# Decay matrices of two token mixers: mask and row spread accumulated on TensorE in three single-pass products, exponentials read from the accumulator bank

## Reference

```python
# mLSTM, per chunk, head and direction
dlog = jnp.where(_causal(t), bt[..., :, None] - bt[..., None, :] + it[..., None, :], -jnp.inf)
m_t = jnp.maximum(m_inter, jnp.max(dlog, -1))
s = jnp.exp(dlog - m_t[..., None]) * jnp.einsum('bnthk,bnshk->bnhts', q, k)
# SSD
seg = jnp.where(_causal(t), at[..., :, None] - at[..., None, :], -jnp.inf)
y = jnp.einsum('bnhts,bnshp->bnthp', jnp.exp(seg) * cb, xdt)
```

## Time and profile before

| | |
|---|---|
| median of 3 runs | 2839.63 us (2838.87 to 2845.24) |
| the profiled execution | 2846.07 us, its span 2844.3 us |
| mean granted TensorE clock | 0.921 of full speed |
| mLSTM rounds, layer 0 | 748.2 to 825.6 us of the span |
| SSD rounds, layer 0 | 962.2 to 1082 us |
| mLSTM rounds, layer 1 | 2140.6 to 2203.1 us |
| SSD rounds, layer 1 | 2317.9 to 2402 us |

### The profile page before, as it was taken

One profiled execution on the slowest core, in us unless ns is written; L12 is line 12 of the kernel. 1 busy time (PEld: TensorE's weight loads), 2 busy tenths in 40 slices (PEclk: granted clock), 3 DMA queues, 4 the chain that ended last, 5 costly groups with the idle time before them and its releaser, 6 DMA issues. The chain is left out here.

```text
span 2844.3 us, 37711 instructions
## 1 busy us (share of the span) xinstructions
PE 2462.7 (87%) x13246; PEld 2249.5 (79%) x13246; DVE 1356.0 (48%) x1923; ACT 1060.0 (37%) x1631; POOL 1394.5 (49%) x604
## 2 busy tenths in 40 slices
PE   5699989898778887799998999899987787789997
PEld 2499988777556676799998999787775767779997
DVE  4554252563655426664326541526455533765424
ACT  4333245334433353253225322452443323243322
POOL 3365545465434674355554555455642322536553
PEclk8799999999878898899999999999997888989999
DMA  8443323233332452233332333233432212214332
GB/s 274 141 140 126 119 96 126 90 127 119 116 109 81 152 162 83 89 109 127 114 124 101 128 110 121 93 108 119 134 111 75 83 65 67 91 66 140 126 116 69
DMA packets 93459, 323.16 MB, mean 114 GB/s; under 512 B 11040, under 2 KB 14368, under 8 KB 92960
## 3 DMA queue, kind: packets, MB, share of 16 engines
q1 hardware_dynamic: 87552, 312.03, 33.3%
q10 hardware_dynamic: 5792, 9.56, 1.0%
HBM read 317.35 MB, written 4.20 MB: 113 GB/s over the span
## 5 line engine op out<-in xcount | busy, mean ns | idle before, releaser
L518 POOL TENSOR_TENSOR wlo<-raw,whi 128x1024 fp32r<-128x1024 f32 (+2 forms) x600 | 1394.3, 2332 | 1417.3 <-ACT whi L972 1355.2
L972 ACT CAST whi<-raw 128x1024 fp32r<-128x1024 f32 (+1 forms) x600 | 615.4, 1036 | 1003.7 <-PE ps L552 666.4
L550 PE MATMUL ps<-h_hi,whi 128*128 128x384 f32 x2224 | 765.6, 344 | 34.6 <-DVE h_lo L2023 13.3
L551 PE MATMUL ps<-h_lo,whi 128*128 128x384 f32 x2224 | 754.4, 339 | 0.0
L552 PE MATMUL ps<-h_hi,wlo 128*128 128x384 f32 x2224 | 754.0, 339 | 0.0
L550 PEld LDWEIGHTS ps<-h_hi,whi 128*128 128x128 f32 x2224 | 427.2, 192 | 45.3 <-DVE h_lo L2023 13.9
L551 PEld LDWEIGHTS ps<-h_lo,whi 128*128 128x128 f32 x2224 | 427.0, 192 | 2.8 <-issue 2.2
L552 PEld LDWEIGHTS ps<-h_hi,wlo 128*128 128x128 f32 x2224 | 426.0, 192 | 0.0
L550 PE MATMUL ps<-act_hi,whi 128*128 128x384 f32 x704 | 242.1, 344 | 11.5 <-DVEq L458 6.0
L552 PE MATMUL ps<-act_hi,wlo 128*128 128x384 f32 x704 | 240.5, 342 | 0.0
L551 PE MATMUL ps<-act_lo,whi 128*128 128x384 f32 x704 | 240.3, 341 | 0.0
(11 more groups left out here) (311 smaller groups left out, 3113.3 us busy)
## 6 DMA issues: line engine op xcount, KB each, us to landing
raw<-in_w_in SPq DMA_DIRECT2D x248, 512.0 KB, 3.4
raw<-in_w_gu SPq DMA_DIRECT2D x176, 512.0 KB, 3.4
raw<-in_w_down SPq DMA_DIRECT2D x64, 512.0 KB, 3.4
raw<-in_w_mod SPq DMA_DIRECT2D x40, 512.0 KB, 4.4
raw<-in_w_down SPq DMA_DIRECT2D x32, 384.0 KB, 2.9
raw<-in_w_branch SPq DMA_DIRECT2D x24, 512.0 KB, 3.4
raw<-in_w_out SPq DMA_DIRECT2D x16, 512.0 KB, 3.5
x<-in_x ACTq DMA_DIRECT2D x1, 1536.0 KB, 6.5
```

Source lines behind the costliest of these rows:

```text
L518: nc.gpsimd.tensor_tensor(wlo[s][:, 0:w], raw[s][:, 0:w], whi[s][:, 0:w].bitcast(F32), ALU.subtract).then_inc(w_split, 1)
L550: mm(out, hi_, xh[:, xc, :], start=start and n == 0, stop=False)
L551: mm(out, hi_, xl[:, xc, :], start=False, stop=False)
L972: act.copy(whi[m][:, 0:w], raw[m][:, 0:w]).then_inc(w_hi, 1)
```

## The change

Three things move. `spread` becomes three products of single-pass type (F32R) accumulated in the bank: the identity by the mask (broadcast over the three blocks), the broadcast identity column by the high part `x_5h` of the rows, and by their low part `x_5l`. `exps` and its buffers `pt` go; `pair` reads the bank and waits for PE, and PE waits for `pair` before it overwrites a bank. The identity and the mask become F32R tiles, filled by two DVE copies at the start, and DVE makes `x_5h` and `x_5l` in "rows". Uses of `ident` elsewhere read the same tile as fp32.

```diff
-        ident = sb("ident", [P, P])
+        ident_r = sb("ident_r", [P, P], F32R)
+        ident = ident_r[:, :].bitcast(F32)
...
-        neg = sb("neg", [P, 2, P])
+        neg = sb("neg", [P, 2, P], F32R)
...
-        (pt0, pt1, pr0, pr1, st0, st1), e3 = region(
-            rows0, *[(n, [P, T]) for n in ("pt0", "pt1", "pr0", "pr1", "st0", "st1")])
+        (x_5h, x_5l, pr0, pr1, st0, st1), e3 = region(
+            rows0, ("x_5h", [P, T], F32R), ("x_5l", [P, T], F32R), *[(n, [P, T]) for n in ("pr0", "pr1", "st0", "st1")])
...
-            def spread(r, rr):
-
+            def spread(r, d, rr):
+
+                out = ps[r % 2][:, 0:T]
                 if r >= 2:
-                    pe.wait_ge(pr_x, r - 1)
-                mm(ps[r % 2][:, 0:T], ident[:, rr:rr + 1].to_broadcast([P, P]), x_5[:, :], start=True,
-                   stop=True).then_inc(pr_bc, 1)
+                    pe.wait_ge(pr_e, r - 1)
+                mm(out.rearrange("p (a b) -> p a b", b=P), ident_r[:, :], neg[:, d:d + 1, :].to_broadcast([P, NT, P]),
+                   start=True, stop=False)
+                row = ident_r[:, rr:rr + 1].to_broadcast([P, P])
+                mm(out, row, x_5h[:, :], start=False, stop=False)
+                mm(out, row, x_5l[:, :], start=False, stop=True).then_inc(pr_bc, 1)
...
             def pair(r, rr):
-                act.wait_ge(pr_x, r + 1)
+                act.wait_ge(pr_bc, r + 1)
...
-                    last = af(pr[r % 2][:, c], pt[r % 2][:, c], ACT.Exp, bias=t_1[:, t, rr:rr + 1])
+                    last = af(pr[r % 2][:, c], ps[r % 2][:, c], ACT.Exp, bias=t_1[:, t, rr:rr + 1])
...
             cp(hmask[:, :, :, :], hmask_in[:, :, :, :])
+            cp(ident_r[:, :], ident_in[:, :])
+            cp(neg[:, :, :], neg_in[:, :, :])
...
                 dve.wait_ge(row_d, 3)
+                step.done()
+                step(cp(x_5h[:, :], x_5[:, :]))
+                step.done()
+                step(tt(x_5l[:, :], x_5[:, :], x_5h[:, :].bitcast(F32), ALU.subtract))
                 dve.wait_ge(row_a, 5)
...
-            def exps(r, d):
-                dve.wait_ge(pr_bc, r + 1)
-                if r >= 2:
-                    dve.wait_ge(pr_e, r - 1)
-                tt(pt[r % 2][:, :].rearrange("p (a b) -> p a b", b=P),
-                   neg[:, d:d + 1, :].to_broadcast([P, NT, P]),
-                   ps[r % 2][:, 0:T].rearrange("p (a b) -> p a b", b=P), ALU.add).then_inc(pr_x, 1)
...
-                exps(0, 0)
                 for r in range(8):
-                    if r < 7:
-                        exps(r + 1, (r + 1) % 2)
                     scores(r, ps[2], r // 2 + 1)
...
-                exps(8, 0)
                 for r in range(16):
                     scores(8 + r, ps[2], 5 + r // 8, 64 + 32 * (r % 2) + r // 2)
-                    if r < 15:
-                        exps(9 + r, (r + 1) % 2)
                     skipped(r)
```

More of the change, by code:

```diff
@@ L201, in build @@
         tb, sbf, vb, sq, ht = (tb0, tb1), (sb0, sb1), (vb0, vb1), (sq0, sq1, sq2, sq3), (ht0, ht1, tb0)
-        (pos, hmask_in), _ = region(arena, ("pos", [P, KC, NL_TOK]), ("hmask_in", [P, 2, len(LEVELS) + 1, P]))
+        (pos, hmask_in, ident_in, neg_in), _ = region(
+            arena, ("pos", [P, KC, NL_TOK]), ("hmask_in", [P, 2, len(LEVELS) + 1, P]), ("ident_in", [P, P]),
+            ("neg_in", [P, 2, P]))
         (mq, mk, va), hg0 = region(arena, ("mq", [P, NH, T]), ("mk", [P, NH, T]), ("va", [P, NT, NH, C1]))
@@ L248, in build @@
         (kw0, kw1), _ = region(e6 - 2 * T * 4, ("kw0", [P, 2, P]), ("kw1", [P, 2, P]))
-        pt, pr, st, kw, co = (pt0, pt1), (pr0, pr1), (st0, st1), (kw0, kw1), (co0, co1)
+        pr, st, kw, co = (pr0, pr1), (st0, st1), (kw0, kw1), (co0, co1)
         (xt, bt), _ = region(e6 - 2 * T * 4 - 2048 - NT * MIX * 4 - 9312, ("xt", [P, NT, MIX]), ("bt", [P, NT, P]))
@@ L339, in build @@
         pr_bc = signal("pe", "pr_bc")
-        pr_x = signal("dve", "pr_x")
         pr_e = signal("act", "pr_e")
@@ L670, in normed @@
                     for g in range(NH):
-                        last = nc.tensor.transpose(ps[2 + t % 2][:, g * P:(g + 1) * P], nyn[:, g, :], ident[:, :])
+                        last = nc.tensor.transpose(ps[2 + t % 2][:, g * P:(g + 1) * P], nyn[:, g, :], ident)
                     last.then_inc(nm_tr, 1)
@@ L704, in keys_turned @@
                         last = nc.tensor.transpose(ps[2 + s % 2][:, g * P:(g + 1) * P],
-                                                   kk[:, d, g, t * P:(t + 1) * P], ident[:, :])
+                                                   kk[:, d, g, t * P:(t + 1) * P], ident)
                     last.then_inc(hg_t, 1)
@@ L749, in rows @@
                         last = nc.tensor.transpose(ps[i % 2][:, t * P:(t + 1) * P], xi[:, t * P:(t + 1) * P],
-                                                   ident[:, :])
+                                                   ident)
                     last.then_inc(tr_pe, 1)
@@ L763, in keys_turned @@
                         last = nc.tensor.transpose(ps[3 + t % 2][:, g * P:(g + 1) * P],
-                                                   mk[:, g, t * P:(t + 1) * P], ident[:, :])
+                                                   mk[:, g, t * P:(t + 1) * P], ident)
                     last.then_inc(tr_pe, 1)
-            def spread(r, rr):
+            def spread(r, d, rr):
+                out = ps[r % 2][:, 0:T]
                 if r >= 2:
-                    pe.wait_ge(pr_x, r - 1)
-                mm(ps[r % 2][:, 0:T], ident[:, rr:rr + 1].to_broadcast([P, P]), x_5[:, :], start=True,
-                   stop=True).then_inc(pr_bc, 1)
+                    pe.wait_ge(pr_e, r - 1)
[4 more added lines that the diff above has]
+                mm(out, row, x_5l[:, :], start=False, stop=True).then_inc(pr_bc, 1)
             def mlstm(l):
@@ L786, in second @@
                        stop=True).then_inc(ml_i2, 1)
-                spread(0, 0)
+                spread(0, 0, 0)
                 head(0)
@@ L793, in mlstm @@
                     if r < 7:
-                        spread(r + 1, 32 * (1 - d) + (r + 1) // 2)
+                        spread(r + 1, 1 - d, 32 * (1 - d) + (r + 1) // 2)
                     if r:
@@ L826, in ssd @@
                     for g in range(4):
-                        last = nc.tensor.transpose(ps[5][:, g * P:(g + 1) * P], xs[:, g, c], ident[:, :])
+                        last = nc.tensor.transpose(ps[5][:, g * P:(g + 1) * P], xs[:, g, c], ident)
                     last.then_inc(tr_pe, 1)
-                    last = nc.tensor.transpose(ps[6][:, 0:P], xs[:, 4, c], ident[:, :])
+                    last = nc.tensor.transpose(ps[6][:, 0:P], xs[:, 4, c], ident)
                     last.then_inc(tr_pe, 1)
@@ L866, in group @@
                     last.then_inc(pr_qk, 1)
-                spread(8, 64)
+                spread(8, 0, 64)
                 group(0)
@@ L872, in ssd @@
                     if r < 15:
-                        spread(9 + r, 64 + 32 * (1 - d) + (r + 1) // 2)
+                        spread(9 + r, 1 - d, 64 + 32 * (1 - d) + (r + 1) // 2)
                     if r == 8:
@@ L980, in ahead @@
                     round_unit(off + (U_BASE[l] // 4 + k // 4), k % 4, width(l, k))
-            for dst, src in ((x, ins["x"]), (pos, ins["pos"]), (hmask_in, ins["hmask"]), (ident, ins["ident"]),
-                             (mean_w, ins["mean_w"]), (neg, ins["neg"]), (keep, ins["keep"]), (sgn, ins["sgn"])):
+            for dst, src in ((x, ins["x"]), (pos, ins["pos"]), (hmask_in, ins["hmask"]), (ident_in, ins["ident"]),
+                             (mean_w, ins["mean_w"]), (neg_in, ins["neg"]), (keep, ins["keep"]), (sgn, ins["sgn"])):
                 act.dma_start(dst[tuple(slice(None) for _ in dst.shape)], src).then_inc(start_loads, 16)
@@ L1632, in hgrn @@
                 flat = lambda a: a.rearrange("p h t -> p (h t)")
-                eye = ident[:, :].unsqueeze(1).to_broadcast([P, NH, P])
+                eye = ident.unsqueeze(1).to_broadcast([P, NH, P])
                 def total(h):
@@ L1794, in rows @@
                 s_(cp(lastw[b96, :], x_3[b96, 2 * P:2 * P + 1]))
-                ts(dlast[:, :], ident[:, :], lastw[:, :], None, ALU.mult).then_inc(row_d, 1)
+                ts(dlast[:, :], ident, lastw[:, :], None, ALU.mult).then_inc(row_d, 1)
                 dve.wait_ge(row_d, 4)
```

## The result

The changed kernel took 2811.64 us (median of 4 runs, 2807.53 to 2812.37), the kernel before 2840.54 beside it: a ratio of 0.9893 (95% interval 0.9876 to 0.9910), 28.9 us less. Predicted were 2817.5 us and a gain of 22.3. The profiled execution took 2811.02 us, its span 2809.2.

A forecast was written before the change was run, and what follows sets the result against it. PE, busy for 87% of the span, was taken as the bound, so other work counts only where PE waits. The terms 9.0 + 7.4 + 3.0 + 1.9 + 1.0 = 22.3 us, from 2839.6, gave 2817.5 us; 8-in-10 range 2806 to 2833.

The forecast's parts named there:

- The waits for st in mLSTM: mLSTM rounds, L803 and L778: PE's waits for scores go because DVE no longer puts exps(r+1) ahead; 9.0 of 9.4 us.
- 10 us from waits: mLSTM rounds: PE waits less, 9.0 us for the scores st and 1 us for kw and cs.
- seven spreads: Spreads on PE at the low clock level: 0.49 us saved each, 3.4 us of the spread's gain.
- a case of 4 in 100: Whole kernel: larger gain, all kw waits gone and PE less often at the low clock, 31 us or more; chance 0.04.
- The spread: PE, all rounds: three single-pass products take 0.52 instead of 0.64 us at full clock; 7.4 us in sum.
- The chain behind the modulation items: SSD, layer 0: without the mask, PE's wait for POOL's low parts ends 0.75 us earlier in four rounds; 3.0 us.
- The waits for st in SSD: SSD rounds, L878: three of five score waits end a chain through the mask and shorten by 0.63 us each; 1.9 us.
- The waits for kw and cs: mLSTM, L808 and L785: kw waits lose about 4 us, cs waits gain about 3; counted as 1 us gained.
- the first (POOL takes back half): mLSTM: kw and hout fall into POOL's runs in more rounds, -8 instead of +1 us, time 2826.5; chance 0.16.
- the second: Spread on PE: the three products cost 0.32 us each, about 5 us of gain left, 2835; chance 0.07.
- the third, a slower kernel: mLSTM: DVE stalls on POOL in nearly every round, up to 2.35 us each, time up to 2850; chance 0.05.

The follow-up runs named there:

- e1: Kernel before, with DVE's mask step of round r+1 moved behind scores and weights of round r in mLSTM; 2834.6 us, ratio 0.9984.
- e5: Kernel before, in mLSTM DVE's mask step moved behind scores and weights, and ACT's weigh(r-1) ahead of the exponentials of round r+1; 2823.9 us, 0.9933.
- e3: Changed kernel, with a DVE copy of the bank to SBUF where the mask step stood, three products kept; 2839.4 us, ratio 1.0000 to the kernel before.
- e11: Changed kernel, with a DVE copy of the bank to SBUF put back in the mLSTM rounds alone; 2828.8 us, ratio 0.9949 to the kernel before.
- e8: Changed kernel, with a DVE copy of the bank to SBUF put back in the SSD rounds alone; 2823.5 us, ratio 0.9934 to the kernel before.
- e9: Changed kernel, ACT casting a modulation unit's first block ahead of the next round's exponentials in SSD; 2808.0 us, ratio 0.9875 to the kernel before.
- e10: Changed kernel, PE spreading the rows of round r+2, not r+1, at the start of SSD round r; 2809.9 us, ratio 0.9880 to the kernel before.
- e2: Changed kernel, with the rows again as one fp32 product behind the mask product; 2822.3 us, ratio 0.9937 to the kernel before.
- e4: Changed kernel, with the mask product issued twice, four products in all; 2823.1 us, ratio 0.9933 to the kernel before.
- e12: Changed kernel, ACT weighing round r-1 (mLSTM) and casting a modulation unit's first block (SSD) ahead of the next exponentials; 2811.2 us, 0.9899 to the kernel before.

## Why the prediction held, and where its steps failed

**The waits for st in mLSTM (9.0 us): the waits went, for another reason.** Of 9.4 us none is left. But the prediction took the wait that ends last before a product for the bound of the round. e1 took the same wait away by DVE's order and got 5 us, because what was late next was the carry: `heads` stood behind `weigh`, and `weigh` behind the exponentials. The change shortens that loop (3.06 to 1.65 us from carry to `heads` in round 2), and e5 shows the whole mLSTM gain without any of its products. Asking what is late next, the prediction looked only at POOL's lock. Of ACT's order it says that `pair` keeps its place with one releaser fewer, and not that `weigh` stands behind it.

**The size in mLSTM.** Predicted were 10 us from waits and a share of the spread; 18.7 us came. The step over e3 divides it. From e3 to the changed kernel, at equal busy time, 12.2 us are the DVE step and its place, for which the 10 us stood; the other 6.4 (139.8 to 133.4) are the cheaper spread and the clock together. By e11, the same rounds at a lower clock in layer 1 (0.76), the parts are 15.5 and 3.1. So the step was sized 2 to 5 us too low. The clock the prediction priced only in seven spreads, and it left the rest to a case of 4 in 100. As a sum over PE, the waits fell by 7.5 (27.6 to 20.1) and the busy time by 11.7 in the two stretches (56.91 to 49.34 and 44.97 to 40.86), at a clock of 0.82 and 0.79 instead of 0.77 and 0.76.

But that sum does not make the shorter busy time worth 11.7 us, for e3 has it too. The same mLSTM rounds ran at other clocks in e8, e9 and e10. PE's busy time was 86.3, 85.9 and 85.9 us instead of 90.2, and the stretches were 118.9, 119.6 and 119.5 us instead of 121.2: about half came through, and the rest turned into waits (22.2, 22.4 and 22.4 us instead of 20.1). Nor is the cheap spread needed for it: in e5, with the fp32 spread, PE's busy time is 89.9 us, and in layer 0 it is lower than in the changed kernel:

```profile
746.65:811.45 64.80, 47.26 (x248) 32.23 (x248) 54.07 (x112) 30.61 (x65) 37.74 (x16) 0.88 0.47 147
```

**The spread (7.4 us): the price was right, the gain came at most in part.** 0.52 us at full clock, as worked out. In mLSTM e5 has the whole gain without it, and in layer 1 the loop hides it (e2, e4). In SSD it counts where the clock is the same (0.27 us between two waits in e3), but the clock took it back there, and e3 as a whole is no faster than the kernel before. What it is worth in the changed kernel no run shows by itself.

**The chain behind the modulation items (3.0 us): right in its place, smaller.** Three of the five waits are 0.98 us instead of 1.65, as forecast, and the fourth of the forecast is 1.31; in all 2.3 us of waiting went, and five new waits of 0.2 us before the gate projections took 1.0 back. e9 confirms the chain: with the cast ahead of the exponentials four waits go. The whole stretch is only 2.2 us shorter. Three of the four intervals between the five waits are 0.6 to 0.9 us shorter; the one in which the clock fell (see e3) is 0.6 us longer.

**The waits for st in SSD (1.9 us): 1.5** (4.9 to 3.4). In layer 1 the stretch shrank by 6.4 us, more than its waits (3.8 to 2.4) and its sixteen spreads (1.9 at full clock) give; the clock rose there from 0.90 to 0.93, and e12 shows that the clock alone moves this stretch by 4 us.

**The waits for kw and cs (1.0 us): -1.9.** `kw` lost 4.1 us, as walked through, but `cs` gained 6.0, not 3. Where from, the timeline shows, with an operation of round 1 on DVE and the product of round 2 that waits:

```profile
758.02 2.28 DVE L1863 TENSOR_TENSOR den<-den,t 128x3 f32<-128x3 f32 x1
...
761.74 0.49 PE L791 MATMUL ps<-cs,mq 128*128 128x129 f32 x2 [2.44 <-DVE cs L1848]
```

An operation on three elements stands 2.28 us beside POOL's subtraction, and the carry, queued behind it, makes PE wait 2.44 us. The prediction counted `kw` and `hout` as the operations that can be caught; `den` can too, and one on three elements had taken 1.68 us in the kernel before.

**The sum.** 22.3 us against 28.9 held in part by luck, because the terms missed in both directions: the spread's 7.4 us came at most in part, and mLSTM gave 18.7 us where 10 and a share of the spread were forecast. (2839.6 less 22.3 is 2817.3; the prediction writes 2817.5.) Of the rivals, the first (POOL takes back half) came in part, 1.9 us instead of 8; the second fell with the 0.17 us distances; the third, a slower kernel, did not come.

**Left open:** what makes the clock fall in SSD of layer 0 in the changed kernel, e3 and e8, and not in the kernel before; how the 3 to 6 us in mLSTM divide between the cheaper spread and the clock; and what the spread is worth in the time of the changed kernel.

## What to carry to other kernels

A wait names its last releaser, not the loop that sets the round: before pricing a step that is removed, follow the round from carry to carry over all engines, and look in each engine's order for what stands behind the step (here the weighing and the casts behind the exponentials). Moving an instruction on one engine often only renames the wait, so add up all waits of the stage, not the one. And where PE changes its clock level, a change can also move the clock of the next stretch, up or down; give that term its own range, and compare kernels where their busy time or clock is equal before you credit a step. PE's shorter busy time is not a gain by itself: here about half of it turned into waits.

## What the hardware showed unexpectedly

The products with a moving side of stride zero cost what others do: 0.17 us for 384 columns at full clock, also accumulating into a bank. One exponential of 128 columns read from the bank took 358 ns in the mLSTM stretch of layer 0, against 391 from SBUF:

```profile
L1221 ACT ACTIVATE pr<-ps,t 128x128 f32<-128x128 f32 x24 | 7.0, 358 | 5.8 <-PE ps L778 5.8
```

DVE stands still beside POOL on three elements as on 128 columns. Which operations are caught can be seen in the least, median and largest duration of lines of the changed kernel:

```profile
L1835 DVE TENSOR_SCALAR kw<-mkt,pr x32: 273/280/2475, 746.1 to 2167.8; 128x128 f32<-128x128 f32 x32
...
L1863 DVE TENSOR_TENSOR den<-den,t x16: 161/164/2282, 758.0 to 2173.4; 128x3 f32<-128x3 f32 x16
L1865 DVE RECIPROCAL den<-den x16: 175/176/177, 760.3 to 2173.6; 128x3 f32<-128x3 f32 x16
...
L1858 DVE TENSOR_TENSOR tmpb<-tmpa,ps x16: 405/412/414, 757.1 to 2172.8; 128x258 f32<-128x258 f32 x16
```

The sum with one operand in the bank (L1858) and the reciprocal were never caught; the maximum of two SBUF operands (L1863) was. The Trainium skill, "SBUF — State Buffer", section "SBUF: two separate sides", names as takers of the lock DVE operations in a two-port mode or with two SBUF inputs; the trace agrees for these lines.
